# Channel tiles of the split input 2112 instead of 2048 bytes apart, in a four-layer decoder trunk

## The reference

```python
def sq_relu_mlp(h, w1, w2):
    a = jax.nn.relu(h @ w1)
    return (a * a) @ w2

def reference(x, positions, norm_mix, norm_mlp, norm_final, ...):
    for i in range(DEPTH):
        kind, j = i % N_MIXERS, i // N_MIXERS
        h = rmsnorm(x, norm_mix[i])
        ...
        x = x + m.astype(x.dtype)
        x = x + sq_relu_mlp(rmsnorm(x, norm_mlp[i]), mlp_w1[i], mlp_w2[i]).astype(x.dtype)
    return rmsnorm(x, norm_final)
```

## Time and profile before

| what | us |
|---|---|
| median of three runs | 1361.15 |
| lowest and highest | 1358.5, 1361.36 |
| the profiled execution | 1360.47 |
| its span, first to last instruction | 1358.7 |
| PE busy with matmuls | 1315.0 |
| PE busy with weight loads (beside the matmuls) | 1151.9 |
| DVE busy | 892.4 |
| ACT busy | 664.0 |

### The profile page before, as it was taken

One profiled execution on the slowest core, in us unless ns is written; L12 is line 12 of the kernel. 1 busy time (PEld: TensorE's weight loads), 2 busy tenths in 40 slices (PEclk: granted clock), 3 DMA queues, 4 the chain that ended last, 5 costly groups with the idle time before them and its releaser, 6 DMA issues.

```text
span 1358.7 us, 18563 instructions
## 1 busy us (share of the span) xinstructions
PE 1315.0 (97%) x7704; PEld 1151.9 (85%) x7704; DVE 892.4 (66%) x1181; ACT 664.0 (49%) x834; POOL 40.3 (3%) x58
## 2 busy tenths in 40 slices
PE   4999999999999999998999999999999999999997
PEld 4888888888899888887998988888888888888886
DVE  4787765555556566556798786766556776666664
ACT  3455554444454544443775554544444555554442
POOL 2000000000000000000101110000000000000000
PEclk9799999999999999999999999999997999999999
DMA  7654275555664475542764444655534243575540
GB/s 224 178 148 153 94 236 202 194 193 183 163 179 166 160 243 190 187 159 93 240 214 152 156 145 131 238 189 191 195 106 180 87 135 121 170 248 186 186 155 31
DMA packets 147828, 230.95 MB, mean 170 GB/s; under 512 B 7651, under 2 KB 116493, under 8 KB 147744
## 3 DMA queue, kind: packets, MB, share of 16 engines
q1 hardware_dynamic: 144896, 221.66, 49.1%
q0 software_dynamic: 2848, 8.10, 2.8%
HBM read 227.08 MB, written 2.65 MB: 169 GB/s over the span
## 4 chain that ended last, share of the span: by engine, by line
PE 84%; DVE 10%; ACT 2%; DMA 2%; issue 1%; POOL 0%; SPq 0%; DVEq 0%; POOLq 0%; ACTq 0%
PE bank L821 15%; PE acc L740 12%; PE acc L741 12%; PE acc L744 11%; PE bank L823 8%; PE bank L535 6%; PE bank L536 6%; PE bank L537 6%; DVE wlo L518 4%; DVE cacc L1669 2%; PE bank L1168 1%; PE bank L940 1%; ACT whi L508 1%; DMA raw<-in_mla_w_in 1%; PE bank L1174 1%
## 5 line engine op out<-in xcount | busy, mean ns | idle before, releaser
L518 DVE TENSOR_TENSOR wlo<-raw,whi 128x2048 fp32r<-128x2048 f32 (+1 forms) x209 | 467.4, 2245 | 162.5 <-ACT whi L508 162.4
L508 ACT ACTIVATE whi<-raw 128x2048 fp32r<-128x2048 f32 (+1 forms) x209 | 388.8, 1871 | 60.4 <-PE acc L744 44.2
L821 PE MATMUL bank<-hsplit,whi 128*128 128x512 f32 x896 | 318.6, 398 | 0.0
L823 PE MATMUL bank<-hsplit,wlo 128*128 128x256 f32 x896 | 251.5, 281 | 0.0
L821 PEld LDWEIGHTS bank<-hsplit,whi 128*128 128x128 f32 x896 | 168.3, 188 | 41.2
L741 PE MATMUL acc<-wlo,uhi 128*128 128x512 f32 x512 | 200.0, 391 | 0.0
L740 PE MATMUL acc<-whi,uhi 128*128 128x512 f32 x512 | 199.6, 390 | 0.0
L823 PEld LDWEIGHTS bank<-hsplit,wlo 128*128 128x128 f32 x896 | 169.2, 189 | 2.2
L535 PE MATMUL bank<-hsplit,whi 128*128 128x256 f32 (+1 forms) x552 | 160.8, 291 | 5.9 <-DVE xn L1699 3.2
L744 PE MATMUL acc<-whi,ulo 128*128 128x512 f32 x512 | 159.2, 389 | 0.0
L536 PE MATMUL bank<-hsplit,whi 128*128 128x256 f32 (+1 forms) x552 | 157.3, 285 | 0.0
(11 more groups left out here) (221 smaller groups left out, 1876.5 us busy)
## 6 DMA issues: line engine op xcount, KB each, us to landing
raw<-in_mlp_w SPq DMA_DIRECT2D x128, 1024.0 KB, 5.5
raw<-in_ssd_w_in SPq DMA_DIRECT2D x18, 1024.0 KB, 5.4
raw<-in_mla_w_o SPq DMA_DIRECT2D x16, 1024.0 KB, 5.0
raw<-in_mla_w_ukv SPq DMA_DIRECT2D x8, 1024.0 KB, 6.4
raw<-in_moba_w_qkv SPq DMA_DIRECT2D x16, 512.0 KB, 7.6
raw<-in_ssd_w_out SPq DMA_DIRECT2D x8, 1024.0 KB, 5.0
raw<-in_mla_w_uq SPq DMA_DIRECT2D x8, 768.0 KB, 8.3
raw<-in_mla_w_in SPq DMA_DIRECT2D x4, 1024.0 KB, 9.1
```

Of the source, the lines that this page charges most:

```text
L508: nc.scalar.activation(whi[:, s, :e], raw[:, s, :e], ACT.Copy).then_inc(w_hi_done[s], 1)
L518: nc.vector.tensor_tensor(wlo[:, s, :e], raw[:, s, :e], whi[:, s, :e].bitcast(F32), ALU.subtract).then_inc(w_split[s], 1)
L821: nc.tensor.matmul(ps, w[0][:, k, n], hsplit[:, k].rearrange("p a n -> p (a n)"), start=k == 0, stop=False)
L823: mm = nc.tensor.matmul(ps[:, 0:SEQ], w[1][:, k, n], hhi[:, k, :], start=False, stop=k == KD - 1)
```

## The change

A tile of `hsplit` gets 16 elements (64 bytes per partition) of unused space behind it, so that tiles lie 2112 bytes apart. `hsplit` becomes a view of the wider buffer, and `hhi` and `hlo` stay views of `hsplit`. All else is as before; buffers allocated behind it move up by 512 bytes.

```diff
-        hsplit = sb("hsplit", [P, KD, 2, SEQ], F32R)
+        hrows = sb("hsplit", [P, KD, 2 * SEQ + 16], F32R)
+        hsplit = hrows[:, :, 0:2 * SEQ].rearrange("p k (a n) -> p k a n", a=2)
         hhi, hlo = hsplit[:, :, 0, :], hsplit[:, :, 1, :]
```

## The result

The changed kernel is faster: 1351.83 us (median of four runs, 1350.7 to 1352.72) against 1359.83 us (1357.96 to 1361.36), a ratio of 0.9941 with a 95% interval of 0.9924 to 0.9959. The profiled execution took 1351.94 us. Lines of the code are one higher than before: L821 is now L822.

What follows compares the result with a forecast made beforehand. The prediction took the stream of matmuls on TensorE, paced by the distance between starts, to bound the kernel. All terms were 0 on a profiled 1360.47 us, so it forecast 1361 us, range 1355 to 1366 us.

Steps and rivals of the forecast that it cites:

- What bounds the kernel: Whole kernel: a stream of TensorE matmuls, timed by the distance between starts; `hsplit` in more than half of 7704.
- Does distance matter now? Three readings say no: Tile-to-weight distances: three profile readings show no cost for the 128, 256, 512 and 1024-byte bits; 64 bytes taken as 0.
- The sign of being wrong that the prediction names: Up-projection pairs: the prediction is wrong if the three-beat rhythm gives way to one that follows the tile number.
- the beat of three: Up-projection pairs: 0.36 us every third pair, 1.06 us per three; claimed to restart with the instruction sequence, not an address.
- The two halves of an up projection: Output halves 512 bytes apart have the same three-pair time, 1.06 us; so moving later buffers by 512 bytes was put at 0.
- The heads of `uq`: `chi` against `uq` slices: heads 1 and 3 sit 256 bytes off, yet 18 matmuls take 120.0 ns each, as `hsplit` does.
- The 32-column loads: Step-size projection: tiles 5, 6 and 7 stand 384, 256 and 128 bytes off their weights, yet run at the lowest, 113.3 ns.
- The drift argument: Load beside stream: their distance drifts about 500 bytes per load, so 64k shifts only when a distance occurs; 0 expected.
- the slack is contention: Faster rival, chance 0.12: new distances end 12.5 ns per up pair and 6.7 ns on 1536 matmuls; 21.5 us, 1340 us.
- a start off a 128-byte line costs: Slower rival, chance 0.10: odd tiles begin mid-fetch in up projections and other `hsplit` matmuls; 8.5 us together, 1370 us.
- Later buffers at 0: `uhi`, `ulo`, `ohi`, `chi` and the rest move up 512 bytes against the weights; claimed cost 0.
- Writes of `hsplit`: ACT's copy L563 and DVE's subtraction L608 write at a 2112-byte step; at most 0.6 us either way, taken as 0.

Runs made afterwards that it cites:

- e4: Against the kernel before: whole split input moved by 32 bytes, tiles 2048 bytes apart, later buffers placed as in the change; 1350.53 us, ratio 0.9941.
- the map: Separate programs, m1 and m2, timing the kernel's matmul patterns alone with the input at many byte distances, weights fixed; up pairs 346.7 to 360.0 ns.
- e3: Against the kernel before: whole split input moved by 64 bytes, tiles 2048 bytes apart, later buffers as in the change; 1352.86 us, ratio 0.9949.
- m1: Not the kernel: its three matmul patterns on random data at many distances, no other engine beside them; up pair 346.7 ns at 0 and 32 bytes.
- m2: As m1, but each pattern entered from 24 down products, in steps down to 4 bytes, also input stationary; up pair 353.3 ns at 0, 346.7 at 32.
- e8: Against the kernel before: split input at 32 bytes for the MLPs and 112 for the mixers, as views of one buffer; 1348.75 us, ratio 0.9926.
- e2: Against the kernel before: only the 512 bytes added in front of the later buffers, tiles still 2048 bytes apart; 1359.17 us, ratio 0.9993.
- e5: Against the kernel before: meant as 16 bytes, but split input and all later buffers stood 32 bytes off against the weights; 1359.30 us, ratio 1.0002.
- e6: Against the kernel before: the whole split input moved by 256 bytes; 1358.52 us, ratio 0.9995.
- e1: The same change measured again beside the kernel before on one chip, five executions; 1351.16 us against 1359.41, ratio 0.9939.

## Why the prediction was wrong, point by point

**What bounds the kernel: right.** The stream of matmuls sets the time over most of the span, and some 5.3 us of the gain are in the distances between their starts; what is left is mostly the clock, of which the prediction has no term. One count was a little high: the matmuls that it lists are 3808 of 7704, just under half, and 3928 with the 96 of 64 columns and the 24 with loads of 32.

**"Does distance matter now? Three readings say no": this step failed**, in each of its three readings, and with it the 0 that the sum has for the stride of the tiles. In its place the runs showed -6.3 us in the small differences of the change. The sign of being wrong that the prediction names came too: in the trace of the kernel after, the beat of three is gone, and the pairs of tiles 1 to 7 of the projection shown above take 345, 350, 343, 349, 346, 348, 354 ns in the first half and 344, 350, 345, 348, 346, 349, 354 ns in the second, which follows the tile number.
- The two halves of an up projection lie 512 bytes apart, two full periods of 256. They could show nothing. The beat of three is, as the prediction said, a rhythm of loads and streams and not a count of addresses. But the conclusion that addresses don't set it was wrong: at the same sequence of instructions, 32 bytes give another beat and 346.9 ns for 352.5 (e4).
- The heads of `uq` lie 256 bytes off each other, one full period. These 18 matmuls were at distance 0 too. So every row with a full load and a distance within one period was at 0, and what I called three tests was one point.
- The 32-column loads did have distances of 128, 256 and 384 bytes, but only 32 columns to load. The row was true (113.3 ns) and said little on full loads; the map has 351.1 ns for an up pair at 128 bytes with full loads and 353.3 at 0.

**The drift argument failed.** It held that within one load all distances occur anyway. e3, e4 and the maps have constant distances and different times. A load doesn't start at a random moment of the stream. In the timeline of e4, with the weight loads (PEld) beside the matmuls:
```profile
190.27 0.39 PE L823 MATMUL bank<-hsplit,whi 128*128 128x512 f32 x1
190.28 0.19 PEld L825 LDWEIGHTS bank<-hsplit,wlo 128*128 128x128 f32 x1
190.50 0.28 PE L825 MATMUL bank<-hsplit,wlo 128*128 128x256 f32 x1
190.50 0.19 PEld L823 LDWEIGHTS bank<-hsplit,whi 128*128 128x128 f32 x1
```
Each load starts 2 to 4 ns after the matmul before it, so the same meeting comes again at each pair.

**The rival "the slack is contention" had the right direction and looked for the cause in the addresses, with a chance of 0.12**. That load and stream contend for something is its reading; the runs show that the times follow the place of an operand with no other engine at work (m1, m2), and not what the two meet at. Its price was some 3 times too high for this change: 12.5 ns a pair were put down and 4.4 came (348.1 against 352.5), 6.7 ns on a 256-column matmul and 1.7 came in the queries (118.3 against 120.0). The price took every tile to the lowest distance between starts. With an extra of 64 bytes the eight tiles are spread over four distances modulo 256 (0, 64, 128, 192), and one in four stays at 0. The floor is real for the queries and keys (113.3 ns in e8, 113.5 in e3); the pair's 340 ns was reached by no run, the lowest with full loads is 346.7. That the rival left out the 480 matmuls of the convolution's projection was right: what they won was given back.

**The rival "a start off a 128-byte line costs" fell for `hsplit`**: tiles at 64 bytes alone (e3) are faster than at 0, by 2.9 us in the up pairs. What is slow is nearer by: 4 and 24 bytes. For down products a move does cost, 226.7 to 233.2 ns at 32 and 64 bytes, but the 128-byte line isn't it: 128 bytes have 232.0.

**The sum.** Later buffers at 0: right (e2). Writes of `hsplit`: ACT and DVE are as busy as before (664.3 and 892.3 us), right. The uncosted term was the down products, +0.6 us for instructions whose operands kept their distance. They are entered from another rhythm and take longer to settle: by the medians over the groups of 24 in each trace, five start-to-start distances lie above the steady 227 ns before and seven after, and the 24 together take 5467 and 5478 ns. e4 has three such and 5454 ns, which is its -0.7 us. That was in no row before.

The Trainium skill, page "TensorE: Matmul & The Clock Gate", section "Step-by-step: what each phase is for", says that the load of the next weights doesn't take bandwidth from the running matmul. Whether it is bandwidth no run here shows, but the two are not independent in time: the same loads and streams take 340.0 to 369.8 ns for three products by place alone, and the measurement decides. The formula of its section "Back-to-back issue gap", weighed in the prediction, would give 325.0 ns for a pair; the lowest here with full loads is 346.7.

**Open.** Why the period is 256 bytes and why 112 bytes suit three products is not shown by any run; neither is what fixes the choice among the rhythms at one distance, nor whether the distance between the two operands or the start of the moved one counts. Why the changed kernel has the higher granted clock is open too. That e8 beats the change is likely by the small differences (-12.8 against -6.4 us, of which 3.5 and 1.0 us were given back), but their intervals overlap.

## What to carry to other kernels

Where TensorE is bound by matmuls with a fresh load before each, the place of the operands is a parameter. In the maps it is worth up to 8% of these matmuls (369.8 against 340.0 ns for three), in this kernel 0.4% of the time for the change's distances and 0.7% for the best arrangement, and it costs a few bytes of padding. Measure a small map with the kernel's own patterns and its own way into them, in steps down to 4 bytes; the good place differs by pattern (0 for the down products, 32 for the up pairs, 112 for three products), and a pad in one buffer moves all buffers behind it, which can cost as much as it wins (e5). The map is a guide and not the kernel: e3 ran faster in one place than its value in the map. Before a row counts as evidence that a parameter doesn't matter, check that it really has another value of it: values that differ by a full period are the same value. And look at the granted clock before a gain of a few microseconds is put down to the change's own mechanism.

## What the runs showed of the hardware

- Start-to-start distances of fp32r matmuls at the full clock, with a full weight load before each, depend on where the streamed or the loaded operand starts within the partition while the other stays, with a period of 256 bytes: 346.7 to 360.0 ns for a pair of 512 and 256 columns, 340.0 to 369.8 ns for three of 256, 226.6 to 233.3 ns for one of 512 (m1, m2; e6 for the period in the trunk).
- A stream of matmuls settles within some ten instructions in a steady rhythm (e8, m2), and at one distance there can be two: 346.7 and 353.3 ns at 0, by what ran before (m1, m2).
- A weight load starts 2 to 5 ns after the start of the matmul before it in these streams (e4, before).
- One program spends 40.6 or 43.2 us of a span of 1350 us at TensorE's half clock (the change and e1), and the kernel before 49.7 us; a difference in the granted clock of 0.002 is 2.7 us without any change in the distances.
